# The first attention layer of a two-block transformer step with the second token tile ahead of the first

## What is computed

```python
def _chunked_relbias_attention(x, g_norm, w_q, rel_table, w_o, k_pad, v_pad):
    q = (_rms_norm(x, g_norm) @ w_q).reshape(b, n_chunks, CHUNK, B_HEADS, B_HEAD_DIM)
    ...
        sc = jnp.einsum('bqhd,bkhd->bhqk', q_c, k_c).astype(jnp.float32) * ATTN_SCALE + bias
        sc = jnp.where(valid, sc, NEG_INF)
        p = jax.nn.softmax(sc, axis=-1).astype(v_c.dtype)
        return jnp.einsum('bhqk,bkhd->bqhd', p, v_c)
    ...
    return o @ w_o
```

## Time and profile before

| | us |
|---|---|
| median of 3 runs | 1284.38 (1281.71 to 1284.8) |
| the profiled execution, its own time | 1284.02 |
| span of the profile | 1282.1 |
| PE busy | 1229.9 (96%) |
| DVE busy | 697.2 (54%) |
| ACT busy | 544.6 (42%) |
| mean granted clock of PE | 0.977 |

### The profile page before, as it was taken

One profiled execution on the slowest core, in us unless ns is written; L12 is line 12 of the kernel. 1 busy time (PEld: TensorE's weight loads), 2 busy tenths in 40 slices (PEclk: granted clock), 3 DMA queues, 4 the chain that ended last, 5 costly groups with the idle time before them and its releaser, 6 DMA issues.

```text
span 1282.1 us, 14894 instructions
## 1 busy us (share of the span) xinstructions
PE 1229.9 (96%) x6231; PEld 1029.8 (80%) x6231; DVE 697.2 (54%) x703; ACT 544.6 (42%) x654; POOL 65.9 (5%) x121
## 2 busy tenths in 40 slices
PE   6998999999999989999998999999999977999998
PEld 5886888888889977888886888888988866788886
DVE  4557365555465746564535654546945756454552
ACT  4534354444355425454424444434656233444341
POOL 4000000000010001000000000002100010000000
PEclk9998999999999979999999999999999897999999
DMA  8752547556486315755644755645651313466550
GB/s 279 260 198 92 172 150 236 176 178 228 133 292 199 99 33 186 238 197 185 221 140 148 221 175 195 218 143 170 220 180 51 99 50 99 140 188 197 197 197 33
DMA packets 147825, 218.46 MB, mean 170 GB/s; under 512 B 5136, under 2 KB 115760, under 8 KB 147632
## 3 DMA queue, kind: packets, MB, share of 16 engines
q1 hardware_dynamic: 144640, 206.69, 48.9%
q0 software_dynamic: 3120, 10.84, 2.5%
HBM read 216.45 MB, written 1.05 MB: 170 GB/s over the span
## 4 chain that ended last, share of the span: by engine, by line
PE 91%; DVE 5%; issue 1%; ACT 1%; DMA 1%; POOL 1%; SPq 0%; DVEq 0%; POOLq 0%; ACTq 0%
PE acc L1638 27%; PE acc L1640 27%; PE acc L1639 27%; PE turn L1631 4%; DVE w_lo L1057 1%; PE acc L2062 1%; DVE xt L1067 1%; DMA raw<-in_a_w_in 1%; PE turn L2040 1%; PE acc L1820 1%; PE turn L1926 1%; DVE xn L1081 1%; PE turn L1800 0%; ACT w_hi L727 0%; PE turn L2011 0%
## 5 line engine op out<-in xcount | busy, mean ns | idle before, releaser
L1057 DVE TENSOR_TENSOR w_lo<-raw,w_hi 128x2048 fp32r<-128x2048 f32 (+1 forms) x196 | 442.3, 2279 | 202.2 <-ACT w_hi L727 202.0
L1638 PE MATMUL acc<-w_hi,xt 128*128 128x512 f32 (+2 forms) x1112 | 437.9, 394 | 11.0 <-DVE xt L1067 8.9
L727 ACT ACTIVATE w_hi<-raw 128x2048 fp32r<-128x2048 f32 (+1 forms) x196 | 368.2, 1907 | 153.9 <-PE acc L1640 125.3
L1640 PE MATMUL acc<-w_hi,xt 128*128 128x512 f32 (+2 forms) x1112 | 430.8, 387 | 0.0
L1639 PE MATMUL acc<-w_lo,xt 128*128 128x512 f32 (+2 forms) x1112 | 430.2, 387 | 0.0
L1638 PEld LDWEIGHTS acc<-w_hi,xt 128*128 128x128 f32 x1112 | 212.1, 191 | 54.9 <-DVE xt L1067 11.1
L1640 PEld LDWEIGHTS acc<-w_hi,xt 128*128 128x128 f32 x1112 | 211.4, 190 | 42.7
L1639 PEld LDWEIGHTS acc<-w_lo,xt 128*128 128x128 f32 x1112 | 212.2, 191 | 39.9
L1638 PE MATMUL acc<-w_hi,ht 128*128 128x512 f32 x352 | 139.6, 397 | 0.0
L1640 PE MATMUL acc<-w_hi,ht 128*128 128x512 f32 x352 | 138.0, 392 | 0.0
L769 ACT ACTIVATE sg<-acc 128x256 f32<-128x256 f32 x88 | 29.0, 382 | 255.3 <-PE acc L1640 255.3
(11 more groups left out here) (247 smaller groups left out, 886.9 us busy)
## 6 DMA issues: line engine op xcount, KB each, us to landing
raw<-in_ffn_w_gate_up SPq DMA_DIRECT2D x88, 512.0 KB, 5.0
raw<-in_ffn_w_down SPq DMA_DIRECT2D x22, 1024.0 KB, 5.1
raw<-in_ffn_wg SPq DMA_DIRECT2D x44, 512.0 KB, 4.1
raw<-in_ffn_wu SPq DMA_DIRECT2D x44, 512.0 KB, 5.1
raw<-in_ffn_wd SPq DMA_DIRECT2D x22, 1024.0 KB, 5.2
raw<-in_a_w_in SPq DMA_DIRECT2D x16, 1024.0 KB, 6.2
raw<-in_w_in SPq DMA_DIRECT2D x10, 1024.0 KB, 5.5
raw<-in_a_w_out SPq DMA_DIRECT2D x8, 1024.0 KB, 5.2
```

Source lines behind the costliest of these rows:

```text
L727: nc.scalar.activation(w_hi[:, u % RING, 0:kt * w], raw[:, u % RAW, 0:kt * w], ACT.Copy).then_inc(s_hi, 1)
L1057: V.tensor_tensor(w_lo[:, u % RING, 0:kt * w], raw[:, u % RAW, 0:kt * w], w_hi[:, u % RING, 0:kt * w].bitcast(F32), ALU.subtract).then_inc ...
L1638: mm(o, lhs[0], rhs[0], start=start, stop=False)
L1640: return mm(o, lhs[1], rhs[0], start=False, stop=stop)
```

## The change

The steps of a head group are listed with tile 1 first: (1, pairs 0 and 1), (1, pairs 2 and 3), (0, all four pairs). A step of tile 1 with the first two pairs needs only one key unit and one query unit, so `scores(0)` waits for two units read in place of four and stands after `kq_tile(2, 0)` in place of `kq_tile(4, 0)`; `scores(3)` likewise waits for six in place of eight. The queues of PE, ACT and DVE for the layer are written out anew. Counts in the waits, the numbering of the `turn` banks and the place where a weight unit counts as used follow from it. The arithmetic is the same.

```diff
     STEPS1 = [(g, t, [4 * g + j for j in js]) for g in range(2)
-              for t, js in ((0, (0, 1, 2, 3)), (1, (0, 1)), (1, (2, 3)))]
+              for t, js in ((1, (0, 1)), (1, (2, 3)), (0, (0, 1, 2, 3)))]
...
-                pe.wait_ge(s_kq, 4 * (g + 1))
+                pe.wait_ge(s_kq, 4 * (g + 1) - 2 * (i % 3 == 0))
...
-                    if (t, half) == (1, 1 - C_O % 2) and k % 2 == 1:
+                    if (t, half) == (1, C_O % 2) and k % 2 == 1:
                         last.then_inc(s_used, 1)
```

The head of ACT's queue, and its tail:

```diff
-            for i in range(4):
+            for i in range(3):
                 read_kq(i)
                 split_to(U_KQ + 5 + i)
             exps(0)
+            read_kq(3)
+            split_to(U_KQ + 8)
             read_kq(4)
+            exps(1)
...
-            exps(3)
             exps(4)
-            high_out(1, 0)
             exps(5)
+            high_out(1, 1)
             high_out(0, 1)
             squares(R_FFN1, 0, X, s_row, 3)
-            high_out(1, 1)
             split_to(U_O + 6)
```

The second half of DVE's queue:

```diff
-            shares(2)
-            shift(3)
-            heads_out(1, 0)
-            split_to(U_O + 4)
             shares(3)
             shift(4)
-            low_out(1, 0)
+            split_to(U_O + 4)
+            shift(5)
+            shares(4)
+            heads_out(1, 1)
+            shares(5)
+            low_out(1, 1)
             heads_out(0, 1)
-            shares(4)
-            shift(5)
             low_out(0, 1)
-            shares(5)
             residual(2, C_O, U_O + 3, 0)
-            heads_out(1, 1)
             scaled(X, R_FFN1, G_FFN1, 0)
-            low_out(1, 1)
             split_to(U_O + 6)
             low_rows(F[1]["norm"], 0, 0)
```

More of the change, by code:

```diff
@@ L240, in build @@
     STEPS1 = [(g, t, [4 * g + j for j in js]) for g in range(2)
-              for t, js in ((0, (0, 1, 2, 3)), (1, (0, 1)), (1, (2, 3)))]
-    N_S1, N_P1, T_O = [banks(2)], [], {}
-    for i in range(6):
-        N_P1.append(banks(2))
[L245 to L253, removed]
+              for t, js in ((1, (0, 1)), (1, (2, 3)), (0, (0, 1, 2, 3)))]
+    N_S1, N_P1, T_O = [], [], {}
+    for i in range(4):
+        N_S1.append(banks(2))
+        if i < 3:
+            N_P1.append(banks(2))
+    T_O[1, 0] = splits(1)
+    T_O[0, 0] = splits(1)
+    N_P1.append(banks(2))
+    for i in (4, 5):
+        N_S1.append(banks(2))
+    for i in (4, 5):
+        N_P1.append(banks(2))
+    T_O[1, 1] = splits(1)
+    T_O[0, 1] = splits(1)
     C_O = blocks(2)
@@ L849, in _ @@
             exps(0)
+            read_kq(3)
+            split_to(U_KQ + 8)
             read_kq(4)
+            exps(1)
             split_to(U_O + 1)
-            exps(1)
             read_kq(5)
+            exps(2)
             split_to(U_O + 2)
-            exps(2)
+            high_out(1, 0)
+            exps(3)
             read_kq(6)
+            high_out(0, 0)
             split_to(U_O + 3)
-            high_out(0, 0)
             read_kq(7)
             split_to(U_O + 4)
-            exps(3)
             exps(4)
-            high_out(1, 0)
             exps(5)
+            high_out(1, 1)
             high_out(0, 1)
             squares(R_FFN1, 0, X, s_row, 3)
-            high_out(1, 1)
             split_to(U_O + 6)
@@ L1221, in heads_out @@
                 rs = rs1[:, t, 8 * g:8 * g + 8]
-                dve.wait_ge(s_exp, 2 * (3 * g + 2 * t + 1))
+                dve.wait_ge(s_exp, 2 * (3 * g + 3 - t))
                 link(V.reciprocal(rs, sum1[:, t, 8 * g:8 * g + 8]))
-                dve.wait_ge(s_pv, 2 * (3 * g + 2 * t + 1))
+                dve.wait_ge(s_pv, 2 * (3 * g + 3 - t))
                 V.tensor_tensor(xn[:, t, g * BLK:(g + 1) * BLK].rearrange("p (h d) -> p h d", d=HEAD),
@@ L1234, in _ @@
                 low_rows(T_Q, 1, t)
-            split_to(U_KQ + 8)
+            split_to(U_KQ + 6)
             dve.wait_ge(s_rel, 1)
             shift(0)
+            split_to(U_KQ + 7)
             shares(0)
+            split_to(U_KQ + 8)
             shift(1)
-            split_to(U_O + 1)
-            heads_out(0, 0)
             shares(1)
             shift(2)
+            split_to(U_O + 1)
+            heads_out(1, 0)
+            shares(2)
             split_to(U_O + 2)
+            shift(3)
+            heads_out(0, 0)
+            low_out(1, 0)
             low_out(0, 0)
             split_to(U_O + 3)
-            shares(2)
-            shift(3)
-            heads_out(1, 0)
-            split_to(U_O + 4)
             shares(3)
             shift(4)
-            low_out(1, 0)
+            split_to(U_O + 4)
[4 more added lines that the diff above has]
+            low_out(1, 1)
             heads_out(0, 1)
-            shares(4)
-            shift(5)
             low_out(0, 1)
-            shares(5)
             residual(2, C_O, U_O + 3, 0)
-            heads_out(1, 1)
             scaled(X, R_FFN1, G_FFN1, 0)
-            low_out(1, 1)
             split_to(U_O + 6)
@@ L1812, in values @@
                 nk = keys_of(t)
-                if g == 1 and i % 3 < 2:
-                    pe.wait_ge(s_o, t + 1)
+                if i in (3, 5):
+                    pe.wait_ge(s_o, 2 - t)
                 for half in range(2):
@@ L1841, in _ @@
                                                         (1, 2): lambda: [turn_rows(T_Q, G_B, t) for t in range(TT)]})
[L1842 to L1846, removed]
+            for e in range(2):
+                kq_tile(0, e)
+            pe.wait_ge(*freed(T_Q[1][0] + 1))
+            for e in range(2):
+                kq_tile(1, e)
+            kq_tile(2, 0)
+            scores(0)
+            kq_tile(2, 1)
+            kq_tile(3, 0)
+            turn_shares(0)
+            kq_tile(3, 1)
+            values(0)
             kq_tile(4, 0)
-            scores(0)
+            scores(1)
             kq_tile(4, 1)
             kq_tile(5, 0)
[L1851 to L1855, removed]
             turn_shares(1)
             scores(2)
+            kq_tile(5, 1)
+            values(1)
+            kq_tile(6, 0)
+            turn_shares(2)
+            scores(3)
             kq_tile(6, 1)
-            values(1)
-            turn_heads_out(0, 0, 1)
+            values(2)
+            turn_heads_out(1, 0, 1)
             kq_tile(7, 0)
+            turn_heads_out(0, 0, 2)
             kq_tile(7, 1)
-            turn_shares(2)
+            turn_shares(3)
             pe.wait_ge(*freed(T_O[0, 0][0]))
[L1865 to L1870, removed]
+            pe.wait_ge(s_kq, 7)
+            out_tile(0, C_O % 2, 0)
             scores(4)
-            turn_heads_out(1, 0, 2)
             values(3)
+            out_tile(0, 1 - C_O % 2, 0)
+            scores(5)
             turn_shares(4)
-            scores(5)
-            turn_heads_out(0, 1, 3)
             values(4)
+            turn_shares(5)
+            turn_heads_out(1, 1, 3)
+            out_tile(1, 1 - C_O % 2, 0)
+            values(5)
+            pe.wait_ge(*freed(T_O[1, 1][0]))
+            out_tile(1, 1 - C_O % 2, 1)
+            turn_heads_out(0, 1, 4)
+            out_tile(1, C_O % 2, 0)
             pe.wait_ge(*freed(T_O[0, 1][0]))
@@ L1880, in _ @@
             out_tile(0, 1, 1).then_inc(s_half, 1)
[L1881 to L1887, removed]
             out_tile(1, C_O % 2, 1)
             turn_rows(F[1]["norm"], G_FFN1, 0)
-            out_tile(1, 1 - C_O % 2, 1)
             ffn(1, G_FFN1, lambda: turn_rows(F[2]["norm"], G_FFN2, 0))
```

## The result

The changed kernel takes 1289.89 us (median of 6, 1288.04 to 1291.96) against 1284.41 before (median of 6). The ratio is 1.0046, 95% interval 1.0033 to 1.0059: slower by 5.5 us. The profiled execution is the slowest of the six, 1291.96 with a span of 1290.2, 2.1 us above the median, so its layer may show somewhat more than the median does.

A forecast was written before the change was run, and what follows sets the result against it. PE, busy 96% of the span, was taken as the bound. Waits and old clock loss net -0.3, plus 4.9 and 2.2 us for clock falls, gave +6.8 on 1284.02: 1290.8, stated as 1291 us, range 1286 to 1295.5.

The forecast's parts named there:

- Part 1: First head group, transposed shares of step 0: PE waits 2.0 us for ACT, then 0.6 for the second bank; 2.6 new.
- Part 2: Rest of the first group and start of the second: shifts, exponentials and reads hidden under key-query products, no new wait.
- Part 3: Ahead of the values of step 4: PE waits 3.0 us, as DVE finishes step 5's shift before copying step 4's shares.
- Part 4: Second head group: earlier waits for `low_out(0, 1)`, `heads_out(1, 1)` and `low_out(1, 1)` go, and 6.06 us with them.
- Part 5: Layer's end, chain to the next FFN: PE waits 6.9 us, 2.1 before the row transposes and 4.8 behind them.
- The sum at the upper clock: Whole layer: new waits of 11.8 us against the 12.1 of before, -0.3, if TensorE's clock stayed up.
- Part 6: Clock falls: 4.9 us at the middle wait, 2.2 at the end; even chance at the first group, 2.5 if so.
- Rival A: The forecast: clock falls at middle and end waits, +6.8 us; with a first-group fall too, +9.3; chance 0.66 together.
- Rival B: Clock holds at the middle wait and falls only at the layer's end: +1.9 us, 1286.3; chance 0.19.
- Rival C: Clock holds everywhere, or the spell left at the end is short: -0.3 to +1 us, about 1284.5; chance 0.08.
- D: Faster: moving this stage makes a low-clock spell in later stages not happen, worth 3.4 to 6.85 us; 1280, chance 0.07.
- all that a new order could take away: Second head group before the change: 6.06 us of waits plus 6.0 from the lower clock, together 12.1 us.

The follow-up runs named there:

- e1_fill: The changed kernel with 44 idle matmuls of 512 columns placed where PE waits; 1283.81 us, ratio 1.0001 to the kernel before.
- e2_early: The changed kernel with the first transposed shares and the values of step 0 each one key-query product later on PE; 1284.57 us, ratio 1.0007 to before.
- e4_end: The changed kernel with two next-layer weight units split ahead of the squares on ACT and the residual on DVE; 1286.97 us, ratio 1.0030 to before.
- e8_fill_mid: The changed kernel with only the 11 idle matmuls ahead of the values of step 4; 1287.49 us, ratio 1.0030 to before.
- e9_fill_end: The changed kernel with only the 8 and 18 idle matmuls around the transposed rows at the end; 1289.57 us, ratio 1.0042 to before.
- e7_before_fill: The kernel before with 15 idle matmuls in its four short waits between 451 and 463 us; 1281.84 us, ratio 0.9983 to before.
- e3_mid: The changed kernel with step 5's scores ahead of an output tile and its shift ahead of a weight unit; 1283.71 us, ratio 1.0001 to before.

## Why the prediction was right, step by step

- **Part 1, the first group.** 2.6 us of waits forecast, 2.3 measured (2.02 + 0.33). The clock fell there, to which I gave even odds and for which 2.5 us stood beside the sum. The spell was 3.4 us long and cost 1.5 us by e1_fill, a little under the lower bound of 1.7. e2_early shows that wait and spell are worth what they seem (4.4 us of its layer, against 2.3 + 1.5) and that nothing takes their place.
- **Part 2, nothing on the rest.** Right: no further wait of PE from 408 to 458 us.
- **Part 3, the copies behind the shift.** 3.0 forecast, 2.80 measured, ended by DVE `pt`.
- **Part 4.** The waits of before are gone. The prediction says that the earlier trace rows is most of them; it is 2.7 of 6.1 us. Another 0.6 is the scores' wait for `xt`, and 1.7 are for ACT's `sc`, of which part 4 says nothing.
- **Part 5, the end.** 2.1 and 4.8 forecast, 2.10 and 4.11 measured, with 4.5 where the transposes ran at the upper clock. e4_end shows the two weight units in the chain.
- **The sum at the upper clock, -0.3.** e1_fill has the waits and no spell; its layer differs from that of before by -0.06 us, its ratio is 1.0001. This was the most exact step, and it is exact in part by luck: the new waits came to 11.4 in place of 11.8, and the slow work of before would have taken more than the 6.0 us that the sum gives it at the upper clock, since PE is not quite twice as fast there (an estimate from the starts 0.43 and 0.23 us apart).
- **Part 6, the clock.** The mechanism is shown by e1_fill, e8_fill_mid and e9_fill_end. The term at the middle was over-sized: I took a spell of 9.8 us, 4.9 lost, from the length of the one before; it was 6.8, and 3.1 were lost (e1_fill and e8_fill_mid). The end was 2.2 forecast, 2.4 measured (e1_fill and e9_fill_end). The sum of the three spells by e1_fill is 5.8 in the median and 7.0 in the layer, where A without the first spell had 7.1 and with it 9.6.
- **The total.** +6.8 forecast, +5.5 measured, +6.95 in the layer of the profiled execution. Rival A came true in its form with a fall at part 1, with shorter spells than I gave it. That +6.8 is so near the layer's +6.95 is luck: the sum leaves out the first spell, 1.5 us, and has 1.8 too much for the second. A's own figure with a fall at part 1 was +9.3.
- **Rival B** fails by the fall at 461.6, which came with one wait of 2.80 us among small work. The Trainium skill, page "TensorE: Matmul & The Clock Gate", section "Why this matters for your kernels", ties the fall to an unbroken idle gap between bursts of matmuls. The fall at 454.1 of the kernel before does not agree with it: e7_before_fill removed that by filling four short waits of 0.6 to 1.2 us, of which two (0.8 and 0.9) lie ahead of the fall. Rival C is excluded by the same rows. D's mechanism was seen, in e9_fill_end, with the other sign.
- **What I had wrong on the way** was to call the 12.1 us of before "all that a new order could take away". More than half of the slow PE work there lay in the shadow of another chain: e7_before_fill gives 2.2 of the 6.0 back. For the forecast it made no difference, since it compared PE's list with its own time.

The prediction also takes 6.8 us for the shortest spell. The trace of before has one of 3.4 us near its start (columns as in the earlier trace rows), so the lower bounds made from 6.8 were too high:

```profile
17.20:20.60 3.40, 3.40 (x10) 2.62 (x9) 3.40 (x4) 1.24 (x2) 2.96 (x8) 0.50 0.95 305
```

Put together: with the clock held in both, the change costs 1.0001 against 0.9983, 2.3 us (layer: 129.92 against 127.28, 2.6). The rest is the clock: by the layers it costs 7.0 us in the changed kernel and 2.7 in the one before, 4.3 more, and with the 2.6 that makes up the 6.95 measured. In the changed kernel it falls three times in place of once, and more of the slow work lies where nothing hides it.

What stays open: how long a spell lasts in a given execution. The same two waits at the end of the layer (2.1 and 4.1 to 4.5 us) gave 10.2 us in the changed kernel and 6.8 in e2_early, e3_mid and e8_fill_mid; the same wait in the middle (2.8) gave 6.8 in the changed kernel and 3.4 in e2_early.

## What to carry to other kernels

Before an order is changed, walk the in-order list of the helper engines from the last event that feeds them to the thing that the busiest engine needs next; here three such walks, with durations from the old trace, gave every new wait within 0.7 us. What a wait costs on TensorE is itself plus a little under half of the PE work in the spell that it may bring (here 7.0 of 16.4 us), and less where that work is in the shadow of another chain (2.7 of 12.0 before). So move one item (a product, a shift, a split) into the wait, and where that can't be done fill it with matmuls into a bank that nobody reads.

## What the hardware showed that I had not expected

- Idle matmuls in waits are worth something by themselves: 44 of them, in 11 us of waits, made the changed kernel 5.8 us faster, and 15 made the kernel before 2.2 us faster.
- A spell at the lower clock can be as short as 3.4 us (406.9 to 410.4 here, begun among transposes and ended among products of 256 columns). A product of 512 columns starts every 0.43 us in a spell and every 0.23 outside it.
- Spells far behind the changed place can lengthen when the stage comes at another moment (13.7 for 10.2 us, twice, in the profiled execution of e9_fill_end), and cost 1.8 us there, a third of the 5.5 under test.
